# Indexer scores two heads at a time, and the final norm of each prompt tile inside the last layer's attention

## The reference

```
h = rms_norm(x, g_norm[l]);  project h into a_q, a_k, a_v, i_q, i_k, i_w, b_q, b_k, b_v, m_q, gate
score = sum over 4 indexer heads of i_w[h] * relu(i_q[h] . i_k) * IDX_SCALE   # one score per query and key
keep the 256 best admissible keys of each query
o_a = attention of 8 heads (2 kv heads) over the kept keys
o_b = sliding-window attention with sinks, 4 heads;  o_m = attention of 4 heads into 256 memory tokens
x = x + (concat(o_a, o_b, o_m) * silu(gate)) @ w_out[l]
```

## Time and profile before

| | us |
|---|---|
| median of 3 runs (lowest, highest) | 1627.69 (1621.57, 1631.33) |
| the profiled execution's own time | 1629.99 |
| its span, first to last instruction | 1628.2 |
| PE busy in it | 1440.5 |
| DVE busy | 903.0 |
| ACT busy | 653.2 |
| POOL busy | 161.9 |
| mean granted PE clock | 0.941 |
| issue of the weights for QUERIES in layer 0 (SP, L537) | at 177.5 |
| a 2 MB weight load, issue to landing, median | 10.0 |
| layer 0: PE idle before NORM's transposes of a memory tile | 2.14, ending at 176.3 |

### The profile page before, as it was taken

How to read it: one execution, slowest core, us unless ns; L and a number is a source line. 1 busy time by engine, 2 the same in 40 slices (tenths; PEclk the granted TensorE clock), 3 DMA queues, 4 the chain that set the end, 5 groups by cost and what they waited for, 6 DMA issues and landing times. The chain is left out here.

```text
span 1628.2 us, 19386 instructions
## 1 busy us (share of the span) xinstructions
PE 1440.5 (88%) x6364; PEld 794.2 (49%) x6364; DVE 903.0 (55%) x2433; ACT 653.2 (40%) x1627; POOL 161.9 (10%) x191
## 2 busy tenths in 40 slices
PE   5999999999868999988699999999995899998882
PEld 3444465666534444443444445566663444544450
DVE  1444627887635676754133453488773457676533
ACT  1133427775614434333112342477665233333322
POOL 1100013300001000000010001132000001000003
PEclk9999799999979999999689997999998999999976
DMA  6101400213142211101241013003312412211106
GB/s 196 52 25 34 159 26 1 104 41 92 53 98 72 78 53 52 49 11 29 67 153 49 25 39 136 26 1 117 75 57 52 131 53 59 53 52 46 33 4 242
DMA packets 122760, 109.65 MB, mean 67 GB/s; under 512 B 56656, under 2 KB 95280, under 8 KB 122672
## 3 DMA queue, kind: packets, MB, share of 16 engines
q1 hardware_dynamic: 122672, 108.51, 22.0%
HBM read 82.81 MB, written 25.78 MB: 67 GB/s over the span
## 5 line engine op out<-in xcount | busy, mean ns | idle before, releaser
L739 PE MATMUL score_ps<-w_slot,hT 128*128 128x512 f32 (+2 forms) x1024 | 388.2, 538 | 7.4 <-DMA w_slot<-in_w_in_dram 5.0
L739 PEld LDWEIGHTS score_ps<-w_slot,hT 128*128 128x128 f32 x1024 | 195.8, 194 | 188.0 <-issue 181.9
L739 PE MATMUL score_ps<-w_slot,work 128*128 128x512 f32 x512 | 240.1, 624 | 25.7 <-issue 25.7
L1103 ACT ACTIVATE hT<-hT,neg_top 128x128 f32<-128x128 f32 (+8 forms) x144 | 116.8, 813 | 321.3 <-DVE neg_top L1375 321.1
L1257 DVE TENSOR_SCALAR_CACHE_REDUCE work<-bias,trial 128x384 f32<-128x384 f32 (+3 forms) x256 | 226.1, 883 | 6.9
L965 ACT ACTIVATE work<-bias,neg_trial 128x768 bf16<-128x768 f32 (+2 forms) x192 | 198.4, 1043 | 67.1 <-DVE neg_trial L1253 67.1
L739 PEld LDWEIGHTS score_ps<-w_slot,work 128*128 128x128 f32 x512 | 99.5, 200 | 154.7 <-issue 154.5
L810 PE MATMUL score_ps<-hT,w_slot 128*128 128x352 f32 x448 | 135.2, 460 | 1.4 <-ACT gate_raw L1087 1.4
L1158 POOL TENSOR_TENSOR work<-work,norm_sb 128x512 f32<-128x512 f32 (+1 forms) x36 | 43.1, 1197 | 882.4 <-DMA norm_sb<-norm_scratch 882.4
L724 PE MATMUL turn_ps<-ident,hT 128*128 128x128 f32 (+1 forms) x720 | 98.1, 276 | 26.6 <-ACT work L1128 18.4
L869 PE MATMUL score_ps<-akT,query_mem 64*128 64x512 f32 (+4 forms) x448 | 105.8, 560 | 8.0 <-ACT prob_bm L1117 6.7
(11 more groups left out here) (181 smaller groups left out, 1744.9 us busy)
## 6 DMA issues: line engine op xcount, KB each, us to landing
w_slot<-in_w_in_dram SPq DMA_DIRECT2D x8, 2048.0 KB, 10.0
gate_raw<-in_x_prompt_dram SPq DMA_DIRECT2D x16, 512.0 KB, 3.7
work<-gate_scratch SPq DMA_DIRECT2D x16, 512.0 KB, 4.7
norm_sb<-norm_scratch SPq DMA_DIRECT2D x64, 128.0 KB, 3.3
x_scratch<-gate_raw SPq DMA_DIRECT2D x16, 512.0 KB, 3.7
gate_raw<-x_scratch SPq DMA_DIRECT2D x16, 512.0 KB, 3.7
gate_scratch<-gate_raw SPq DMA_DIRECT2D x16, 264.0 KB, 3.1
gate_scratch<-gate_raw SPq DMA_DIRECT2D x8, 528.0 KB, 2.7
```

The source lines that it names most:

```text
L739: last = nc.tensor.matmul(out[:, 0:cols], lhs(k), w[:, k, 0:cols], start=(k == 0), stop=(k == KD - 1))
L1103: ins = nc.scalar.activation(p, p, ACT.Exp, bias=neg, scale=SM_SCALE, accum_out=sums[t % 2][0:r, col:col + 1])
```

## The change

**Index.** A step is now two heads (a pair `hp`) over one piece `c` of 512 keys. The two multiplications use the two halves of the contraction rows and write the two halves of one score buffer. ACT does one relu per head and piece, DVE one addition per head and piece. The list has 2 steps for tiles of 384 and 512 keys, 4 for 640 to 1024, 6 for the sample; steps stand in the same slots as far as there are any. The waits for stored keys move from ACT to DVE's TOPK.

**Final norm.** In the last layer FINAL_RSTD of tile t-1 follows its ADD: ACT squares, POOL makes rstd. FINAL multiplies on DVE in the third group of A1 of tile t (the last one where there are only two). SP's `x_store` waits for FINAL and stores to the output. The closing block keeps the sample alone. `g_final` is loaded early in the last layer.

```diff
 def attention_steps():
...
                 steps.append(("ADD", t - 1, c))
+                if c:
+                    steps.append(("FINAL_RSTD", t - 1))
+                    finals.append(("FINAL", t - 1))
...
                 held.clear()
+            if finals and g == min(groups - 1, OUT_AT[0][1][2] + 2):
+                steps.append(finals.pop(0))
             if g == 0:
                 steps += waiting
...
-    return steps + [s for t, c in ((NT - 1, 1), (SMP, 0)) for s in (("OUT", t, c), ("ADD", t, c))]
+    return steps + [("OUT", NT - 1, 1), ("ADD", NT - 1, 1), ("FINAL_RSTD", NT - 1), ("OUT", SMP, 0),
+                    ("FINAL", NT - 1), ("ADD", SMP, 0)]
...
+def index_steps(t):
+    return [("INDEX", t, hp, c) for hp in range(IDX_HEADS // 2) for c in range(-(-NKEYS[t] // 512))]
...
-        index = [("INDEX", t - 2, h) for h in range(IDX_HEADS) if t - 2 in SEARCHED]
+        index = index_steps(t - 2) if t - 2 in SEARCHED else []
         steps += [("SQUARE", t + 2), ("KEYS", t)] + index[0:1] + [("NORM", t + 2)] + index[1:2]
...
-    steps += [("INDEX", NT - 1, h) for h in range(IDX_HEADS)] + [("KEYS_T", SMP)]
+    steps += index_steps(NT - 1) + [("KEYS_T", SMP)]
+    last = index_steps(SMP)
     for h, filler in enumerate([("QUERIES", 0), ("MEM", 0), ("MEM", 1)]):
-        steps += [filler, ("INDEX", SMP, h)]
-    steps.append(("INDEX", SMP, IDX_HEADS - 1))
+        steps += [filler] + last[2 * h:2 * h + 2]
...
                     def x_store(t):
+                        if layer == DEPTH - 1 and t < SMP:
+                            sp.wait_ge(final_made, t + 1)
+                            sp.dma_start(y_prompt[0, t * P:(t + 1) * P, :], x_sb[t % 2][:, :]).then_inc(x_stored[t % 2], 16)
+                            return
...
 (PE)
+                            for u in range(2):
+                                half = slice(HD * u, HD * (u + 1))
+                                last = nc.tensor.matmul(out[0:r, 512 * u:512 * u + w],
+                                                        iqT[half, hp, t * P:t * P + r],
+                                                        ikT[half, k0:k0 + w], start=True, stop=True)
...
 (ACT)
                             if u >= 2:
-                                act.wait_ge(score_added, u - 1)
+                                act.wait_ge(score_added, 2 * (u - 1))
+                            for k in range(2):
+                                at = slice(512 * k, 512 * k + w)
+                                ins = nc.scalar.activation(index_relu[u % 2][0:r, at], ps[0:r, at], ACT.Relu,
+                                                           scale=iw_abs[0:r, t, 2 * hp + k:2 * hp + k + 1])
...
+                        elif kind == "FINAL_RSTD" and layer == DEPTH - 1:
+                            t = step[1]
+                            for c in range(2):
+                                scores_taken(act, ("OUT", t, c))
+                            nc.scalar.activation(final_square[:, :], x_sb[t % 2][:, :], ACT.Square,
+                                                 accum_out=sumsq[:, t:t + 1]).then_inc(final_squared, 1)
...
 (POOL)
+                        elif kind == "FINAL_RSTD" and layer == DEPTH - 1:
+                            pool.wait_ge(final_squared, t + 1)
+                            nc.gpsimd.tensor_scalar(meansq[:, t:t + 1], sumsq[:, t:t + 1], 1.0 / D_MODEL, EPS,
+                                                    ALU.mult, ALU.add).then_inc(final_mean, 1)
+                            pool.wait_ge(final_mean, t + 1)
+                            nc.gpsimd.tensor_tensor(rstd[:, t:t + 1], meansq[:, t:t + 1], half_neg[:, 0:1],
+                                                    ALU.pow).then_inc(final_rstd, 1)
...
 (DVE)
+                            scores_taken(dve, step)
+                            s = bias[0:r, KEY_OFF[t] + 512 * c:KEY_OFF[t] + 512 * c + w]
+                            for k in range(2):
+                                if (hp, k) == (0, 0):
+                                    ins = nc.vector.tensor_scalar(s, rl, sign, None, ALU.mult)
+                                else:
+                                    ins = nc.vector.scalar_tensor_tensor(out=s, in0=rl, scalar=sign, in1=s,
+                                                                         op0=ALU.mult, op1=ALU.add)
+                                signal(ins, score_added, 2 * u + k + 1)
...
+                        elif kind == "FINAL" and layer == DEPTH - 1:
+                            t = step[1]
+                            dve.wait_ge(final_rstd, t + 1)
+                            x = x_sb[t % 2][:, :]
+                            nc.vector.scalar_tensor_tensor(out=x, in0=x, scalar=rstd[:, t:t + 1], in1=g_final_sb[:, :],
+                                                           op0=ALU.mult, op1=ALU.mult).then_inc(final_made, 1)
```

More of the change, by code:

```diff
@@ L240 @@
 SCORE_USE, TURN_USE, ATT_GROUP = numbered(STEPS)
+INDEX_STEPS = [s for s in STEPS if s[0] == "INDEX"]
 QK_DONE = [s[1:] for s in STEPS if s[0] == "QK" and ends_scores(*s[1:])]
@@ L361, in hybrid_stream_kernel @@
         rope_loaded = sem("rope_loaded")
-        last_loaded = [sem(f"last_loaded{t}") for t in range(TILES)]
+        last_loaded = sem("last_loaded")
+        last_stored = sem("last_stored")
+        final_loaded = sem("final_loaded")
         first_sem.clear()
@@ L824, in _ @@
                                     turn_taken(pe, ("KEYS_T", t), 1)
-                            r, half, k0 = ROWS[t], HD * (h % 2), 0 if t < SMP else SEQ
+                            r, k0 = ROWS[t], (0 if t < SMP else SEQ) + 512 * c
+                            w = min(512, NKEYS[t] - 512 * c)
                             out = score_buffer(step)
[L827 to L837, removed]
+                            for u in range(2):
[3 more added lines that the diff above has]
+                                                        ikT[half, k0:k0 + w], start=True, stop=True)
                             last.then_inc(score_full, 1)
@@ L1040, in _ @@
                         elif kind == "INDEX":
[L1041 to L1043 removed]
+                            t, hp, c = step[1:]
+                            r, w, u = ROWS[t], min(512, NKEYS[t] - 512 * c), INDEX_STEPS.index(step)
                             ps, free = scores(step)
                             act.wait_ge(iw_done, t + 1)
[L1046 to L1049, removed]
                             if u >= 2:
[L1051 to L1054 removed]
+                                act.wait_ge(score_added, 2 * (u - 1))
[3 more added lines that the diff above has]
+                                                           scale=iw_abs[0:r, t, 2 * hp + k:2 * hp + k + 1])
                             ins.then_inc(free, 1)
[L1056 to L1059, removed]
                         elif kind == "QUERIES":
@@ L1333, in _ @@
+                            if hp == IDX_HEADS // 2 - 1 and 512 * c + w == n and t < SMP:
+                                link(nc.vector.memset(s[0:CHUNK, w - CHUNK:w], NEG))
                         elif kind == "TOPK":
+                            for b in range(2):
+                                dve.wait_ge(kv_stored[b], 16 * kv_dmas(b, TILES))
                             for t in range(TILES):
@@ L1460, in hybrid_stream_kernel @@
             nc.all_engine_barrier()
-        g_final_sb = bias[:, 0:D_MODEL]
-        last_x = [hT[:, D_MODEL * t:D_MODEL * (t + 1)] for t in range(NT)] + [x_sb[0]]
+        last_x = gate_raw[1][0:DEC, 0:D_MODEL]
         with nc.Block() as block:
@@ L1490, in _ @@
+                nc.scalar.activation(square_out[0:DEC, :], last_x, ACT.Square,
+                                     accum_out=sumsq[0:DEC, SMP:SMP + 1]).then_inc(square_done, 1)
             @block.gpsimd
             def _(pool):
-                for t in range(TILES):
-                    r = ROWS[t]
-                    pool.wait_ge(square_done, t + 1)
-                    nc.gpsimd.tensor_scalar(meansq[0:r, t:t + 1], sumsq[0:r, t:t + 1], 1.0 / D_MODEL, EPS,
-                                            ALU.mult, ALU.add).then_inc(mean_done, 1)
-                    pool.wait_ge(mean_done, t + 1)
-                    nc.gpsimd.tensor_tensor(rstd[0:r, t:t + 1], meansq[0:r, t:t + 1], half_neg[0:r, 0:1],
-                                            ALU.pow).then_inc(rstd_done, 1)
+                pool.wait_ge(square_done, 1)
@@ L1504, in _ @@
-                for t in range(TILES):
-                    r = ROWS[t]
-                    dve.wait_ge(rstd_done, t + 1)
-                    nc.vector.scalar_tensor_tensor(out=last_x[t][0:r, :], in0=last_x[t][0:r, :],
-                                                   scalar=rstd[0:r, t:t + 1], in1=g_final_sb[0:r, :],
-                                                   op0=ALU.mult, op1=ALU.mult).then_inc(x_added, 1)
+                dve.wait_ge(rstd_done, 1)
```

(3 more changed lines are left out.)

71 lines of the change are left out of this document (32 added, 39 removed).

## The result

| | us, median | ratio to the kernel before, 95% interval |
|---|---|---|
| before | 1627.8 | |
| changed | 1642.9 (1635.3 to 1647.4, 8 runs) | 1.0086 (1.0057 to 1.0116) |

The account below looks back on a forecast made before the run. PE, busy 88%, was taken as the engine to relieve. Index 0, closing block -18.4, norm's cost +28 gave +9.6 us on the profiled 1630.0: 1639.6, so a median of 1637; 8-in-10 range 1615 to 1652.

Parts of the forecast that it names:

- index tile 4, gap: Short index tile with steps of 512 and 128 keys: gap 7.65 us against 7.7, so no change.
- end of the index stage: From KEYS 7 to QUERIES 0: pairs halve PE's time, ROPE starts earlier; -5.5 us, from -7 to -2.
- falls of the clock, KEYS 5 to 7 and QUERIES 0: Index stage: new PE waits bring about 2.4 clock falls a layer at some 1.9 us; +4.5, bounds 0 and 8.
- idle before FINAL, tiles 1 to 7: Last attention: DVE stands at FINAL for POOL's rstd, which is behind GATE_SCALE and its DMA; 24.6 us in all.
- layer 1's attention: The moved norm's cost in the last attention, mainly DVE waiting for POOL: +28 us, between 9 and 34.
- The correction of -3: Last attention: 3 us taken off PE's summed lateness of 27.6 for PE waits that would have come anyway.
- the falls of +3.4: Last attention: 3.4 us added for two falls of the clock in waits over 4 us.
- Rival (a): At DVE's FINAL: the norm is absorbed, PE sees only 9 us of work, the tail gives 18.4; 1618 us, chance 0.16.
- (b): Clock holds in short index tiles, end of stage gains 7: -9 us there, norm as forecast; 1628, chance 0.14.
- (c): Index pairs pay by PE's share, half of what they save, -20 us and more: 1617 or less, chance 0.04.
- (e): Index pairs do not overlap, PE at 2.2 us per step, +5 or so at stage end: 1647, chance 0.04.
- (d): Falls of the clock spread through the attention after every wait: +14 us more, 1651, chance 0.08.

Follow-up runs that it names:

- the adds later: DVE's index adds of tiles 2 to 6 moved behind the KEYS_T copies: 0.9932 on the kernel before, 0.9838 on that kernel with paired index heads.
- the pairs alone: Kernel before with only the index part (pairs of heads), final norm in the closing block as before: 1631.1 us, ratio 1.0013.
- FINAL behind MIX: Changed kernel with FINAL of tiles 0 to 6 moved on DVE to right after MIX of the same item: 1607.6 us, ratio 0.9877.
- the norm part alone with rstd ahead: Kernel before plus the final norm change only, single index heads, FINAL_RSTD ahead of GATE_SCALE on POOL: 1609.6 us, ratio 0.9888.
- The run with the norm part alone: Kernel before plus the final norm change only, index heads one at a time: 1645.3 us, ratio 1.0098.
- the run without POOL's rstd: Changed kernel with FINAL scaling by a constant 1 and waiting only for ACT's square, not POOL: 1609.1 us, ratio 0.9918.

## Why the prediction was right

By its own steps, the profiled executions beside each:

| step | forecast, us | measured |
|---|---|---|
| index tile 3, gap | +1.1 | +1.6 / +1.6 |
| index tile 2, gap | +1.0 | +1.4 / +1.4 |
| index tile 4, gap | 0 | +0.4 / +1.4 |
| end of the index stage | -5.5 | -3.5 / -5.3 |
| sample's heads | -1.0 | -1.0 / -1.0 |
| falls of the clock, KEYS 5 to 7 and QUERIES 0 | +4.5 | +5.3 / +1.6 |
| both index stages | 0 | +3.9 |
| closing block | -18.4 | -18.6 |
| idle before FINAL, tiles 1 to 7 | 24.6 | 25.2 |
| layer 1's attention | +28 | +29.5 |
| in it, PE standing | +24.6 (27.6 - 3) | +20.5 |
| in it, falls of the clock | +3.4 | +9.0 |

**The mechanism.** The forecast put the loss at FINAL, in a wait for POOL's rstd behind a GATE_SCALE that waits for a DMA. Three runs that take the wait away by three different means (POOL's order, another operand, DVE's order) bring the attention back to within 0.1 to 4.9 us of before. That is shown, not only read. In the seven profiles where the FINALs inside the attention wait 0.2 us or less, the attention takes 327.1 to 335.5 us, 331.2 in the mean; in the four kernels without FINAL there it takes 328.8 to 330.6, 329.9 in the mean.

**Tile by tile.** PE's lateness in the seven tiles was forecast as 4.7, 5.5, 3.0, 5.0, 5.0, 3.0, 1.4 and is 9.9, 5.3, 3.4, 5.5, 4.1, 1.9, -1.7. Tile 1 is mis-sized. The step said "Behind it are a copy, one QK, both MIX". The profile shows M's top there as well. The step had put FINAL behind it, at 1292.35, the end of the row. With it came ACT's exponentials and the copies behind them. So DVE reached FINAL sooner, waited 8.0 instead of 6.2, and PE lost the whole wait and more. Tile 7 was forecast without a wait: DVE waited 2.5 us there, and PE was not later for it. The other five waited 2.8, 3.2, 3.6, 4.3 and 0.9, less than forecast.

**The correction of -3 and the falls of +3.4** were both too small. The windows of layer 1's attention, kernel before and changed kernel (columns as in the earlier trace rows):

```profile
1265.70:1596.30 330.60, 299.82 (x1636) 155.48 (x1636) 192.03 (x508) 112.90 (x297) 19.08 (x16) 0.95 0.19 52
```

```profile
1270.00:1630.10 360.10, 308.85 (x1636) 162.45 (x1636) 199.51 (x516) 122.29 (x313) 24.64 (x32) 0.90 0.17 46
```

PE works 9.0 us longer on the same 1636 instructions, at a mean granted clock of 0.90 instead of 0.95, and stands 20.5 us longer. So 4 us less of the loss is standing, and 6 us more is the clock, than was forecast. That the sum came within 1.5 us of the +28 is in part luck: these two misses and those of the tiles run against each other. The whole forecast is 6 us short of what was measured, 9.3 against 15.2. In the profiled executions, where it was 9.6, the index stages are 3.9 of the 5.6 us that are missing and layer 1's attention 1.5. The index sum also has a slip of sign, since 1.0 + 1.1 - 5.5 - 1.0 + 4.5 is +0.1; it was taken as nothing, so nothing hangs on it.

**The index.** DVE's order was the right reason, and the earlier trace rows the right row. What the step missed is in tile 4: 7.65 was taken against 7.7, and PE lost 0.4 us in layer 0, at a granted clock of 1.00, and 1.4 in layer 1, at 0.81. In this order the pairs gave nothing. With the adds later they gave 20.6 us of index stages (263.0 - 242.4), and 0.94% by the ratios (0.9932 - 0.9838), some 15 us. The read-out's place in DVE's queue was the bound, not its amount: DVE did the same instructions in both. The page TensorEngine Tiling (Array Packing) of the Trainium skill (Performance Considerations, PSUM Bottleneck) says that tiling speeds TensorE but not the read-out of its results, which may then become the bottleneck. The runs agree for the order of the change, with a ratio of 1.0013 for the pairs alone, and not for the other, with the 0.94% above.

**Rival (a)** said that PE would see only FINAL's work, 9 us. Its condition did not hold in the change, but with the wait gone PE does not see even that: +0.1 with FINAL behind MIX and +1.2 in the means above, so most of the 7 x 1.28 = 9.0 us of DVE work is hidden, and the lower bound of 9 us was too high. **(b)** failed at its place: the clock did not hold. **(c)** and **(e)** are not seen: PE takes 1.13 us for a pair over 512 keys, at 121.71 in tile 3's timeline above. **(d)**, falls of the clock after every wait with +14 more, is seen in part: the falls cost layer 1's attention 9.0 us, 5.6 more than the forecast's 3.4. In its first four tiles the granted clock is 0.82 to 0.92, where it was 0.94 to 1.00.

**What is left open.** Over the fourteen profiles the first attention, whose work no edit touches, takes from 325.4 to 333.5 us. The shortest has a mean granted clock of 0.955 there, the longest 0.943 and others down to 0.936. The change itself is 15 us, so single profiles are read to some 5 us, and why this stage varies was not tried.

## To carry to other kernels

When a change gives an in-order engine a wait for another in-order engine, look at what stands ahead of the signal on that second engine, and put the signal ahead of anything that waits for a DMA, or put the waiting instruction behind one that waits for the same thing already. When one engine gets quicker by pairing and nothing improves, look at the order, not the amount, of the work on the engine that reads its results: what frees the first engine goes first, what nobody waits for goes beside the next long stage. Test with the two edits alone and together, since here each alone gave 0 and 0.7%, and both 1.6%.

## What the runs showed of the hardware

**The clock falls on identical work.** In the norm part alone with rstd ahead, index tile 4 of layer 0 has the same instructions and waits as the kernel before. The windows of the gap, this run and then the kernel before (columns as above):

```profile
137.90:148.70 10.80, 10.53 (x36) 6.09 (x35) 3.63 (x8) 5.04 (x16) 0.00 (x0) 0.67 0.00 0
```

```profile
138.90:146.60 7.70, 7.27 (x36) 4.41 (x35) 3.63 (x8) 5.04 (x16) 0.00 (x0) 1.00 0.00 0
```

At a mean granted clock of 0.67 (part of it at the lower level, 1.2 GHz) the gap takes 10.8 us, at 1.00 it takes 7.7, and KEYS 7 behind it 14.7 and 13.2. Ahead of the fall PE had not stood longer than before: its wait for DVE there is 0.27 us in both timelines. So an estimate of falls, like mine of 4.5 us a layer, is good to some 4.6 us a layer (3.1 + 1.5). The run with the norm part alone shows the same fall at the same place.

**DVE and POOL hold each other up.** Both FINAL (1.28 us alone) and GATE_SCALE (1.27 alone) read two inputs from SBUF. With rstd ahead of GATE_SCALE, or without POOL's rstd, the two often meet. One such place in the norm part alone with rstd ahead, DVE's row, then POOL's:

```profile
1363.45 1.28 DVE L1489 SCALAR_TENSOR_TENSOR gate_raw<-gate_raw,rstd,g_final_sb 128x1024 f32<-128x1024 f32 x1
...
1363.57 2.30 POOL L1200 TENSOR_TENSOR work<-work,norm_sb 128x512 f32<-128x512 f32 x1 [3.62 <-DMA norm_sb<-norm_scratch]
```

FINAL keeps its time and GATE_SCALE takes 1 us more. Of this there are eleven cases in four runs, with GATE_SCALE 0.12 to 0.97 us behind FINAL's start. GATE_SCALE takes 1.44 to 2.30 us in them, and ends each time 2.40 to 2.41 us behind FINAL's start, however early it began. So next to nothing of it runs beside FINAL. Spans on POOL are rough in such a profile, but these eleven agree to 0.02 us. What GATE_SCALE's lateness costs was not tried apart. Twice GATE_SCALE began within 0.04 us of FINAL, and then it was FINAL that took longer. One of them, in the run without POOL's rstd; the meansq behind, 0.19 elsewhere, took 1.05 and ended with FINAL:

```profile
1540.36 2.39 DVE L1479 SCALAR_TENSOR_TENSOR gate_raw<-gate_raw,one,g_final_sb 128x1024 f32<-128x1024 f32 x1
...
1540.39 1.27 POOL L1189 TENSOR_TENSOR work<-work,norm_sb 128x512 f32<-128x512 f32 x1 [21.47 <-DMA norm_sb<-norm_scratch]
1541.75 1.05 POOL L1177 TENSOR_SCALAR meansq<-sumsq 128x1 f32<-128x1 f32 x1
```
